# Attention in a hybrid encoder layer: value products that stream 96 columns instead of 64

## The reference, cut to what matters

```
def neighborhood_attention(q, k, v, rpb):
    ...
        s = jnp.einsum('bhnqd,bhrnkd->bhnqrk', q_b, k_blk).astype(jnp.float32)
        ...
        s = s + bias[None]
        p = jax.nn.softmax(s.reshape(B, H, n_blk, NA_QBLK, kh * NA_KBLK), axis=-1).reshape(s.shape)
        o = jnp.einsum('bhnqrk,bhrnkd->bhnqd', p.astype(v.dtype), v_blk)
```

## Time and profile before

| | |
|---|---|
| median of three runs | 3151.77 us (3150.91 to 3152.88) |
| the profiled execution | 3150.39 us, its span 3148.6 us |
| PE busy | 3063.0 us, 97% of the span |
| PEld, DVE, ACT, POOL busy | 2599.7, 1390.3, 862.6, 549.9 us |
| mean granted clock of TensorE | 0.987 |

### The profile page before, as it was taken

How to read it: one execution, slowest core, us unless ns; L and a number is a source line. 1 busy time by engine, 2 the same in 40 slices (tenths; PEclk the granted TensorE clock), 3 DMA queues, 4 the chain that set the end, 5 groups by cost and what they waited for, 6 DMA issues and landing times. The chain is left out here.

```text
span 3148.6 us, 49491 instructions
## 1 busy us (share of the span) xinstructions
PE 3063.0 (97%) x16480; PEld 2599.7 (83%) x16480; DVE 1390.3 (44%) x3181; ACT 862.6 (27%) x1832; POOL 549.9 (17%) x633
## 2 busy tenths in 40 slices
PE   7999999999998999999999999969999997999999
PEld 3888888888885888888888888869999986888887
DVE  5333343433335333333333333326666664555554
ACT  3232322323233111111111111115675671111111
POOL 1111111111112630000000000002333322222221
PEclk9999999999999999999999999989999998999999
DMA  7445444444537732222221222247698646666664
GB/s 288 148 138 169 140 141 152 154 144 137 170 127 299 263 114 82 80 78 82 82 81 70 78 81 81 83 150 215 196 258 248 213 139 198 205 206 203 201 204 141
DMA packets 208757, 491.04 MB, mean 156 GB/s; under 512 B 23275, under 2 KB 85739, under 8 KB 204165
## 3 DMA queue, kind: packets, MB, share of 16 engines
q1 hardware_dynamic: 199255, 462.64, 44.8%
q0 software_dynamic: 9424, 27.43, 2.7%
HBM read 306.83 MB, written 191.00 MB: 158 GB/s over the span
## 5 line engine op out<-in xcount | busy, mean ns | idle before, releaser
L321 PE MATMUL proj<-w_att_hi,a_h_hi 128*128 128x512 f32 x2560 | 1024.1, 400 | 12.7 <-DVE a_h_lo L422 7.1
L321 PE MATMUL proj<-w_att_hi,a_h_lo 128*128 128x512 f32 x2560 | 1001.7, 391 | 0.0
L321 PE MATMUL proj<-w_att_lo,a_h_hi 128*128 128x512 f32 x2560 | 1000.0, 391 | 0.0
L321 PEld LDWEIGHTS proj<-w_att_hi,a_h_hi 128*128 128x128 f32 x2560 | 483.0, 189 | 106.4 <-DVE a_h_lo L422 7.4
L321 PEld LDWEIGHTS proj<-w_att_hi,a_h_lo 128*128 128x128 f32 x2560 | 481.9, 188 | 102.9
L321 PEld LDWEIGHTS proj<-w_att_lo,a_h_hi 128*128 128x128 f32 x2560 | 483.3, 189 | 92.3
L1451 PE MATMUL o_bank<-v_strip,probs_T 120*128 120x64 f32 (+2 forms) x2112 | 278.5, 273 | 14.7 <-ACT probs_T L1300 9.3
L1451 PEld LDWEIGHTS o_bank<-v_strip,probs_T 120*128 120x128 f32 (+2 forms) x2112 | 265.5, 193 | 29.9 <-ACT probs_T L1300 14.6
L1254 POOL CAST q_block<-q_strip 128x512 fp32r<-128x512 f32 x80 | 49.1, 613 | 1283.8 <-DMA q_strip<-q_d 971.1
L1756 PE MATMUL o_proj<-w_out_hi,o_m_hi 128*128 128x512 f32 x640 | 256.6, 401 | 2.5 <-DVE o_m_lo L1677 2.5
L1756 PE MATMUL o_proj<-w_out_hi,o_m_lo 128*128 128x512 f32 x640 | 253.1, 396 | 0.0
(11 more groups left out here) (141 smaller groups left out, 3645.2 us busy)
## 6 DMA issues: line engine op xcount, KB each, us to landing
k_strip<-kT_d SPq DMA_DIRECT2D x12, 1920.0 KB, 11.3
a_x<-in_x SPq DMA_DIRECT2D x40, 512.0 KB, 4.4
a_xT<-in_xT SPq DMA_DIRECT2D x40, 512.0 KB, 5.3
h_d<-a_h_hi SPq DMA_DIRECT2D x40, 512.0 KB, 2.7
h_d<-a_h_lo SPq DMA_DIRECT2D x40, 512.0 KB, 3.4
kT_d<-k_parts SPq DMA_DIRECT2D x80, 256.0 KB, 3.5
q_strip<-q_d SPq DMA_DIRECT2D x40, 512.0 KB, 6.8
o_x<-in_x SPq DMA_DIRECT2D x40, 512.0 KB, 4.0
```

The lines of the kernel that those rows point to most:

```text
L321: last = self.nc.tensor.matmul(bank, h[:, par, k, :], w[:, n, k, :], start=(k == 0 and j == 0), stop=(k == KB - 1 and j == 2))
```

## The change

Each value product streams 96 columns of v_strip instead of 64: the head's own 64 and 32 of its neighbour's. Heads 0 and 2 take the first half of the head on their right, heads 1 and 3 the second half of the head on their left. Each head has 96 columns of the o_bank, 384 of the bank's 512. The scaling on DVE reads only the heads' own 64 columns, which lie in pairs of blocks at columns 0 to 63 and 128 to 191 of each 192. The number of instructions and their order on every engine stay as they are. The lines of the kernel behind the new constant move down by one, and those behind the scaling by two.

```
+V_WIDE = 96
...
-                nc.vector.tensor_tensor(out[:, u // COLS % 2, u % COLS].rearrange("p (h d) -> p h d", h=GH),
-                                        o_banks[u % 2][:, 0:GW].rearrange("p (h d) -> p h d", h=GH),
-                                        inverse[:, u % 2, :].unsqueeze(2).to_broadcast([P, GH, NHD]),
-                                        ALU.mult).then_inc(scaled, 1)
+                nc.vector.tensor_tensor(out[:, u // COLS % 2, u % COLS].rearrange("p (i j d) -> p i j d", i=2, j=2),
+                                        o_banks[u % 2][:, 0:GH * V_WIDE]
+                                        .rearrange("p (i j d) -> p i j d", i=2, j=3)[:, :, 0:3:2, :],
+                                        inverse[:, u % 2, :].rearrange("p (i j) -> p i j", i=2).unsqueeze(3)
+                                        .to_broadcast([P, 2, 2, NHD]), ALU.mult).then_inc(scaled, 1)
...
-                cols = slice(h * NHD, (h + 1) * NHD)
+                to, at = slice(h * V_WIDE, (h + 1) * V_WIDE), h * NHD - h % 2 * (V_WIDE - NHD)
...
-                    last = nc.tensor.matmul(o_banks[u % 2][:, cols], probs_T[0:group, j % 2, c, :],
-                                            v_strip[0:group, u // COLS, slots[c], cols],
+                    last = nc.tensor.matmul(o_banks[u % 2][:, to], probs_T[0:group, j % 2, c, :],
+                                            v_strip[0:group, u // COLS, slots[c], at:at + V_WIDE],
```

## The result

The changed kernel takes 3155.8 us (median of 20 runs, 3151.21 to 3159.23) against 3151.13 us for the kernel before (20 runs, 3147.29 to 3152.88). The ratio is 1.0015 with a 95% interval of 1.0008 to 1.0022: a small loss, 4.7 us, clear of zero; its middle lies inside the 0.2% that I had called no change, and the interval reaches a little past it. The forecast was 5.4 us more.

A forecast was written before the change was run, and what follows sets the result against it. PE was taken to bound the attention stage, with weight loads setting the value rows' distance. 201 delays of 27 ns gave 5.4 us, 3151.77 + 5.4 = 3157.2 us, with a range from 3150 to 3165 us.

The forecast's parts named there:

- What bounds: Attention stage: PE sets the pace; value rows start 0.112 us apart, set by weight loads, with column streams lying under them.
- The middle of a run: Value rows inside a run: 32 more columns stay under the next load, which comes every 112 ns; cost 0.
- The last row in front of a turn: Last value row of a run: its 80 ns stream delays the turn by 27 ns.
- How often: Turns behind value runs: 239 delays, less 19 x 2 swallowed by waits for ACT, leaves 201; 5.4 us in all.
- The scaling: DVE's scaling, reading strided blocks of 64 columns: stays at 425 ns, cost 0.
- The sum: Whole kernel: 5.4 us more, 3157.2 us on the scale of the runs, 0.17% more.
- Every product paying for its columns: Rival, all 2112 value rows: each pays 27 ns, 57 us in all, 3209 us; chance 0.08.
- A shorter stretch of the lower clock: Rival, attention stage: wider streams bring the full clock back earlier, up to 5.6 us, net 3151.6 us; chance 0.13.
- The slower scaling: Rival, DVE's scaling: the strided read is slower and comes through, 5.4 + 8 = 13.4 us, 3165 us; chance 0.05.
- the loss that is not seen at all: Rival, run ends: the turn is held by something else, the tail costs 0, 3152 us; chance 0.14.

The follow-up runs named there:

- the move with 96: Changed kernel (96 columns) with the next unit's first turn issued between the values of heads 2 and 3: 3141.44 us against 3150.59, ratio 0.9969.
- the layout alone: Kernel before with only the changed bank layout and strided scaling, products streaming their own 64 columns: 3151.18 us against 3150.59, ratio 1.0002.
- the turn ahead: Kernel before with the next unit's first turn issued between the values of heads 2 and 3: 3137.64 us against 3150.59, ratio 0.9953.

## Why the prediction was right, point by point

**What bounds.** The reading that something other than the columns sets the distance of the value rows held. It rested on 64 and 128 columns at one distance; the runs put 96 and 128 columns of the very same products at that distance, and 192 columns at 0.163 us. That the distance is the length of the load is argued and not shown: every value product loads 128 columns, no run changed that, and a fixed step of 112 ns for each load and product would look the same in the middle of a run.

**The middle of a run costs nothing.** Shown by narrowing only the rows in front of a turn: 0.06 us left of 4.62.

**The last row in front of a turn.** This term was right in kind and slightly too large: 27 ns were taken, 24.4 were measured. The two readings gave 22 (by the turn's load) and 27 (by the stream alone), and the truth lies between. From 96 to 128 columns another 51.9 - 24.4 = 27.5 ns came on top, so there the full stream is paid. This fits a turn that waited 2 or 3 ns for its own load with 64 columns, so that the first ns of a longer stream went into that, and the traces bear it out. The first row of a turn behind a value product lasts 276.2 ns in the mean of the 71 units with 64 columns, and 274.0 with 96 and 274.1 with 128. The difference goes with the size of the turn's load: 279.2 against 272.8 ns (64 against 96 columns) where the load has 128 columns, 276.0 against 274.3 with 120, and none with 96.

One reading under this term does not stand. I took the recorded starts of the last value row (2304.71) and of the turn (2304.82) as a sign that the turn starts "about as early as this allows", that is 53 to 58 ns after the stream begins. They lie 0.112 us apart, and do so with 96 and 128 columns as well, so they could not show it. That load and stream were nearly level came out right; the sizes from the durations carried it, not this row.

**How often.** The 201 places of the whole stage are not read one by one, but the 189 of the 71 units give the same price for 96 columns (24.4 ns), for the move with 96 (24.5 on 260 places) and, with 128, the price that the stream asks for. The swallowed delays are seen in the wait for ACT, 0.21 us instead of 0.26. In the trace with 128 columns, too, the 12 units with that wait grew by about one delay and the other 59 by about three.

**The scaling** cost nothing, alone (ratio 1.0002) and in the changed kernel (424 ns).

**The sum.** 201 x 24.4 ns = 4.9 us, against 4.7 measured between the medians and 5.4 predicted.

**The rivals.** Every product paying for its columns would have put the turn at 0.75 us; it is at 0.64. That rival becomes true only where the stream outlasts the load, as with 192 columns. The Trainium skill's sentence that throughput is purely the columns streamed (TensorE: Matmul & The Clock Gate, "Step-by-step: what each phase is for") describes this kernel with 192 columns, where the columns set the distance of 0.163 us a row, and not with 64 to 128, where it is 0.112 whatever the width. One column per cycle, as that section of the Trainium skill has it, would be 0.080 us for 192 columns at 2.4 GHz, an estimate; the rows here take twice that. A shorter stretch of the lower clock did occur after the change, but the layout alone with 64 columns shows it as well, so wider columns are not needed for it. I had said that the stretch would end near 2126.5 us; it ended near 2127 and had begun later. The slower scaling and the loss that is not seen at all are both out.

## What to carry to other kernels

Before a wider stream is priced, ask what sets the distance between the rows: two widths with one distance in the trace say that it is not the columns (here most likely the load of the stationary operand), and then columns are free until their stream outlasts it (here somewhere between 128 and 192 of float32). Look at the last row of each run by itself, since what follows may have a shorter load, and count which of these delays a later wait swallows. A wait between two runs can be filled with other work of the same engine (here a turn), and its true length is the distance to the start that the run would have had, not to the usual distance of rows.

## What the runs showed of the hardware that was not expected

After the wait for ACT near the end of the stage (1.7 us in one piece) the clock went to its lower level for a time that differs between the profiled executions: 3.4 us before, 6.8 us with the turn ahead, and not at all with 128 columns, where the wait was 1.66 us. The wait before, then the first and the last of these as stretches (columns as above):

```profile
2562.28 1.79 PE L1451 MATMUL o_bank<-v_strip,probs_T 128*128 128x64 f32 x12 [1.70 <-ACT probs_T L1300]
...
2563.40:2566.90 3.50, 3.50 (x18) 3.50 (x18) 1.77 (x3) 2.07 (x4) 0.00 (x0) 0.51 0.00 0
```

```profile
2560.00:2580.00 20.00, 17.42 (x136) 16.17 (x134) 12.28 (x38) 15.31 (x33) 6.15 (x6) 1.00 0.38 124
```

The last seven units took 45.12 us before and 46.39 with the turn ahead. The kernel with 128 columns, whose tails cost 10 us in all, thus lost nothing to the clock there. With 192 columns the clock did not fall there either, but there the longest such wait is 0.89 us. A second wait of 1.69 us, at 2588.57, was not followed by a fall before the change; one of 1.68 us, at 2593.56, was followed by one after it. With one profile for each kernel it stays open whether wider streams help to hold the clock or whether this is chance; the layout alone and the changed kernel do not differ in the first stretch.
